# TensorE's instruction stream of a two-layer hybrid decoder: FFN loops written out, and one gate row moved to another PSUM bank

## What is computed

```python
c_act = jax.nn.silu(c)
for l in range(DEPTH):                                   # DEPTH = 2
    mod = (c_act @ ada_w[l] + ada_b[l]).reshape(bsz, 3, 3, D_MODEL)
    h = _modulated_norm(x, norm_g[l, 0], mod[:, 0, 0], mod[:, 0, 1])
    x = x + MACARON_WEIGHT * mod[:, 0, 2][:, None, :] * _swiglu(h, ffn1_w_in[l], ffn1_w_out[l])
    h = _modulated_norm(x, norm_g[l, 1], mod[:, 1, 0], mod[:, 1, 1])
    mix = _token_mixer(h, positions, mix_w_in[l], ...)   # three gated branches
    x = x + mod[:, 1, 2][:, None, :] * mix
    h = _modulated_norm(x, norm_g[l, 2], mod[:, 2, 0], mod[:, 2, 1])
    x = x + MACARON_WEIGHT * mod[:, 2, 2][:, None, :] * _swiglu(h, ffn2_w_in[l], ffn2_w_out[l])
return _rms_norm(x, final_norm_g)
```

## Time and profile before

| | |
|---|---|
| three executions without the profiler | median 1522.95 us (1521.99 to 1523.3) |
| the profiled execution | 1519.81 us, of it span of the instructions 1518.0 us |
| TensorE matmul busy | 1377.5 us (91%), 11953 matmuls |
| VectorE busy | 1014.2 us (67%) |
| ScalarE, GpSimd busy | 650.8 us (43%), 229.5 us (15%) |
| TensorE's share of the chain that ended last | 74% |
| mean granted TensorE clock | 0.975 of full speed |

### The profile page before, as it was taken

One profiled execution on the slowest core, in us unless ns is written; L12 is line 12 of the kernel. 1 busy time (PEld: TensorE's weight loads), 2 busy tenths in 40 slices (PEclk: granted clock), 3 DMA queues, 4 the chain that ended last, 5 costly groups with the idle time before them and its releaser, 6 DMA issues.

```text
span 1518.0 us, 28716 instructions
## 1 busy us (share of the span) xinstructions
PE 1377.5 (91%) x11953; PEld 1272.9 (84%) x11953; DVE 1014.2 (67%) x1327; ACT 650.8 (43%) x943; POOL 229.5 (15%) x256
## 2 busy tenths in 40 slices
PE   1899999978899999999989999897888999999997
PEld 1899978967689988999879998796777898799986
DVE  5777768557555776776677676765656378757756
ACT  2443335465623435443353333536364243643433
POOL 2123200030030001232003230102101100022300
PEclk9999999999999999999999999999899999999999
DMA  8998875824302856997769896792441085599852
GB/s 291 308 291 260 297 259 172 228 56 121 102 4 83 279 167 197 266 267 255 247 205 285 247 299 238 223 243 63 111 112 30 3 241 214 165 273 272 276 208 99
DMA packets 354073, 301.81 MB, mean 199 GB/s; under 512 B 19871, under 2 KB 295344, under 8 KB 353968
## 3 DMA queue, kind: packets, MB, share of 16 engines
q1 hardware_dynamic: 353968, 300.36, 65.7%
HBM read 299.28 MB, written 1.05 MB: 198 GB/s over the span
## 4 chain that ended last, share of the span: by engine, by line
PE 74%; DVE 13%; ACT 6%; DVEq 3%; issue 2%; DMA 1%; ACTq 1%; SPq 0%
PE PS L1520 16%; PE PS L1468 15%; PE PS L1470 14%; PE PS L1469 14%; DVE wl L914 3%; DVE ada_acc L1002 3%; ACT wh L603 3%; PE PS L1891 2%; PE PS L1550 2%; DVE x L961 1%; DMA raw<-in_mix_w_in 1%; DVEq L987 1%; PE PS L1557 1%; PE PS L1510 1%; DVEq L960 1%
## 5 line engine op out<-in xcount | busy, mean ns | idle before, releaser
L603 ACT ACTIVATE wh<-raw 128x1024 fp32r<-128x1024 f32 (+1 forms) x400 | 396.6, 1038 | 604.7 <-PE PS L1470 428.0
L914 DVE TENSOR_TENSOR wl<-raw,wh 128x1024 fp32r<-128x1024 f32 (+1 forms) x400 | 474.2, 1226 | 260.4 <-ACT wh L603 260.4
L1468 PE MATMUL PS<-h_hi,wh 128*128 128x256 f32 x2128 | 608.3, 286 | 26.5 <-DVE h_lo L936 14.1
L1469 PE MATMUL PS<-h_lo,wh 128*128 128x256 f32 x2128 | 600.1, 282 | 0.0
L1470 PE MATMUL PS<-h_hi,wl 128*128 128x256 f32 x2128 | 599.6, 282 | 0.0
L1468 PEld LDWEIGHTS PS<-h_hi,wh 128*128 128x128 f32 x2128 | 409.4, 192 | 31.4 <-issue 24.5
L1469 PEld LDWEIGHTS PS<-h_lo,wh 128*128 128x128 f32 x2128 | 411.3, 193 | 0.6 <-issue 0.5
L1470 PEld LDWEIGHTS PS<-h_hi,wl 128*128 128x128 f32 x2128 | 408.8, 192 | 0.0
L1002 DVE SCALAR_TENSOR_TENSOR ada_acc<-ada_w_ring,cact,ada_acc 128x512 f32<-128x512 f32 x280 | 217.9, 778 | 23.8 <-issue 0.9
L1374 POOL CAST hid_hi<-hf 128x256 fp32r<-128x256 f32 x88 | 64.9, 738 | 432.6 <-DVE hf L973 432.6
L1520 PE MATMUL PS<-wh,hid_hi 128*128 128x512 f32 x320 | 101.8, 399 | 0.0
(11 more groups left out here) (306 smaller groups left out, 1568.3 us busy)
## 6 DMA issues: line engine op xcount, KB each, us to landing
raw<-in_ffn_w_in SPq DMA_DIRECT2D x176, 512.0 KB, 5.4
ada_w_ring<-in_ada_w SPq DMA_DIRECT2D x160, 512.0 KB, 5.2
raw<-in_mix_w_in SPq DMA_DIRECT2D x90, 512.0 KB, 6.4
raw<-in_ffn_w_out SPq DMA_DIRECT2D x44, 1024.0 KB, 5.9
raw<-in_branch_w SPq DMA_DIRECT2D x8, 1024.0 KB, 8.2
raw<-in_mix_w_out SPq DMA_DIRECT2D x8, 1024.0 KB, 4.9
gate_row<-in_ada_b SPq DMA_DIRECT2D x6, 512.0 KB, 6.8
raw<-in_mix_w_in SPq DMA_DIRECT2D x2, 1024.0 KB, 6.2
```

The source lines that it names most:

```text
L603: nc.scalar.activation(wh[:, s % 2, h * n:(h + 1) * n], raw[:, s % 4, h * n:(h + 1) * n], ACT.Copy).then_inc(*one("w_hi"))
L914: V.tensor_tensor(wl[:, s % 2, h * n:(h + 1) * n], raw[:, s % 4, h * n:(h + 1) * n], wh[:, s % 2, h * n:(h + 1) * n].bitcast(F32), ALU.sub ...
L1468: M(out, wh[(slice(None),) + wsl], rhs_h, start=start, stop=False, skip_group_check=True)
L1469: M(out, wh[(slice(None),) + wsl], rhs_l, start=False, stop=False, skip_group_check=True)
```

## The change

TensorE's part of `ffn` is written as a plain `for` over all 22 steps, so `steps`, `still`, the offset `o` and the multiplier `times` are gone everywhere. All waits and addresses on TensorE become constants, and the executed matmuls and their order stay the same. On the other four engines the functions lose an argument that was always zero; their instructions stay as they were, row for row. Beside that, `gate_sum(14)` writes bank 0 in place of bank 4 and loses its wait for `ya_final`.

```diff
-GATE_ROW_BANK = {9: 3, 10: 3, 14: 4, 15: 4, 20: 3, 21: 3}
+GATE_ROW_BANK = {9: 3, 10: 3, 14: 0, 15: 4, 20: 3, 21: 3}
...
-        def steps(eng, first, count, peel=0, tail=0):
...
-            rounds = (count - peel - tail) // 4
-            at0 = first + peel
-            times[0] = rounds
-            with eng.Fori(0, rounds) as i:
-                for u in range(4):
-                    yield at0 + u, lambda n: i * n
-            times[0] = 1
...
-            def split_ready(s, half, o, l):
-                pe.wait_ge(*at("w_split", 2 * s + half + 1 + o(8), l))
+            def split_ready(s, half, l):
+                pe.wait_ge(*at("w_split", 2 * s + half + 1, l))
...
-            def ada_sum(gr, l, o=still, inc=one):
+            def ada_sum(gr, l, inc=one):
 
                 col = ADA_COL.get(gr, 4 * (gr % 16))
-                pe.wait_ge(*at("ada_used", 4 * gr + 4 + o(4), l))
+                pe.wait_ge(*at("ada_used", 4 * gr + 4, l))
                 for i in range(4):
-                    ins = M(PS[:, 7, bass.ds(o(4) + col + i, 1)], acc[:, i * P:(i + 1) * P], onecol,
+                    ins = M(PS[:, 7, col + i:col + i + 1], acc[:, i * P:(i + 1) * P], onecol,
                             start=True, stop=True)
...
-                for s, o in steps(pe, s0, KF, peel=(2, 6)[f]):
-                    j = s - s0
-
-                    pe.wait_ge(*at("hf_ready", f * KF + j - 3 + o(4), l))
+                for j in range(KF):
+                    s = s0 + j
+                    pe.wait_ge(*at("hf_ready", f * KF + j - 3, l))
                     if j == 0:
                         ins = first_slot(s, 0, f * 2 * KD, l)
                     for half in range(2) if j else ():
-                        split_ready(s, half, o, l)
+                        split_ready(s, half, l)
                         ins = in_tile(s, half, j % 4, half * T)
                     ins.then_inc(*one("w_used"))
                     if f == 0 and j % 4 == 0 and j >= 4:
-                        ada_sum(3 + j // 4, l, o)
+                        ada_sum(3 + j // 4, l)
...
                     if j == 9:
-                        pe.wait_ge(*at("ya_final", 1, l))
                         gate_sum(14, l)
```

More of the change, by code:

```diff
@@ L345, in hybrid_trunk @@
         tally.clear()
-        times = [1]
         def sem(name):
@@ L365, in at @@
             return sem(name), l * per_layer.get(name, 0) + v
-        def still(n):
-            return 0
-        def steps(eng, first, count, peel=0, tail=0):
-            if eng is not nc.tensor:
-                for s in range(first, first + count):
-                    yield s, still
-                return
-            for s in range(first, first + peel):
-                yield s, still
-            rounds = (count - peel - tail) // 4
-            at0 = first + peel
-            times[0] = rounds
-            with eng.Fori(0, rounds) as i:
-                for u in range(4):
-                    yield at0 + u, lambda n: i * n
-            times[0] = 1
-            for s in range(at0 + 4 * rounds, first + count):
-                yield s, still
         def ada_place(n, l):
@@ L462, in ffn_loads @@
                         row_loads((l + 1) % DEPTH, j - 4)
-                for s, o in steps(sp, s1, 11, peel=1, tail=2):
-                    j = s - s1
-                    free(s, o, l)
-                    sp.dma_start(rows(s, 2), wout[f][:, bass.ds(l * KF + 2 * j + o(8), 2), :])\
+                for j in range(11):
+                    s = s1 + j
+                    free(s, l)
+                    sp.dma_start(rows(s, 2), wout[f][:, bass.ds(l * KF + 2 * j, 2), :])\
                         .then_inc(sem(f"raw_loaded{s % 4}"), 16)
                     if f == 0 or 1 <= j <= 8:
-                        ada((36, 79)[f] + j, o, l)
+                        ada((36, 79)[f] + j, l)
                     if f == 0 and j == 0:
@@ L534, in _ @@
             for n in range(4):
-                ada(n, still, 0)
+                ada(n, 0)
             sp.dma_start(x[:, :, :], a["x"][0].rearrange("(t p) d -> p t d", p=P)).then_inc(sem("x_loaded"), 16)
@@ L570, in _ @@
                     if s < RW_IN:
-                        ada(47 + s - ATT_IN, still, l)
+                        ada(47 + s - ATT_IN, l)
                 for j in range(12):
                     s = GATE_IN + j
-                    free(s, still, l)
+                    free(s, l)
                     for half in range(2):
@@ L582, in _ @@
                     for n in ADA_LOADS.get(j, ()):
[L583 removed]
+                        ada(n, l)
                 for s in range(BRANCH, FFN2_IN):
[L585 removed]
+                    free(s, l)
                     w, k0, per = (wbr, 2 * (s - BRANCH), 9) if s < MIX_OUT else (wmo, 2 * (s - MIX_OUT), KD)
@@ L676, in _ @@
                     vectors(l)
-                    round_w(0, still, l)
+                    round_w(0, l)
                 norm(l, 0, 1)
@@ L975, in ffn, with ada @@
                     if f == 0 or 4 <= j < 20:
-                        ada((16, 60)[f] + j, o, l)
-                for s, o in steps(dve, s1, 11, peel=1, tail=2):
-                    j = s - s1
+                        ada((16, 60)[f] + j, l)
+                for j in range(11):
+                    s = s1 + j
                     if j < 9:
-                        split(s + 2, o, l)
+                        split(s + 2, l)
                     if 1 <= j <= 8:
-                        ada((37, 79)[f] + j, o, l)
-            def ada(n, o, l, inc=one):
+                        ada((37, 79)[f] + j, l)
+            def ada(n, l, inc=one):
                 q = n % 4
                 dve.drain()
-                dve.wait_ge(sem(f"ada_loaded{q}"), l * (18 * 16) + 16 * (n // 4 + 1) + o(16))
+                dve.wait_ge(sem(f"ada_loaded{q}"), l * (18 * 16) + 16 * (n // 4 + 1))
                 if q == 0 and n:
-                    dve.wait_ge(*at("acc_used", n // 4 + o(1), l))
+                    dve.wait_ge(*at("acc_used", n // 4, l))
                     if n // 4 - 1 in (9, 10, 14, 20):
@@ L1035, in _ @@
             for n in range(16):
-                ada(n, still, 0, inc=once)
+                ada(n, 0, inc=once)
             for l in range(DEPTH):
@@ L1292, in _ @@
                 for j in range(6, 12):
-                    split(GATE_IN + j + 2, still, l)
+                    split(GATE_IN + j + 2, l)
                     for n in ADA_SUMS[j]:
-                        ada(n, still, l)
+                        ada(n, l)
                 dve.wait_ge(*at("gate_ready", 12, l))
@@ L1331, in _ @@
                 merge(2, 0)
-                split(MIX_OUT, still, l)
+                split(MIX_OUT, l)
                 merged_lo(0)
@@ L2002, in _ @@
                     s = BRANCH + kb // 2
-                    split_ready(s, kb % 2 if kb < 8 else 1, still, l)
+                    split_ready(s, kb % 2 if kb < 8 else 1, l)
                     if n == 1 and k == 0:
```

192 lines of the change are left out of this document (95 added, 97 removed).

## The result

The changed kernel is slower. Over 22 executions of each its median is 1527.31 us (1522.17 to 1531.15) against 1521.83 us (1515.44 to 1528.63) for the kernel before; the ratio is 1.0031, 95% interval 1.0019 to 1.0043, that is 4.7 us where a gain of 1.8 was forecast. The profiled execution of the changed kernel took 1527.76 us, its span 1526.0, against 1519.81 and 1518.0. In the new program `mm3` is L1443 to L1445, `ada_sum` L1525, `gate_sum` L1532, `ada` L977, the rounding to `wh` L578, the rest `wl` L889.

What follows compares the result with a forecast made beforehand. TensorE's own stream, its matmuls busy 91% of the span, was taken as the bound; 1.6 us from the `ada_sum` waits plus 0.2 from the gate row made 1.8, median 1522.95 to 1521.2 us, range 1516.0 to 1527.5.

Steps and rivals of the forecast that it cites:

- rival A: Matmuls behind `ada_sum`: more rounds run at the slow pace, 0.63 us net each, median 1529.5 us; chance 0.12 that it shows.
- Branches and register additions: TensorE's feed-forward loops: removing these instructions gains nothing, since matmuls keep their ordinary pace across a branch.
- rival C: TensorE's loops: each of 14 backward branches did cost a 1.0 us fetch, 14 us gained, 1507.1 us; chance 0.04.
- Rival D: DVE's next `ada` is timed by something other than TensorE, so the 0.09 us is given back: 1522.8 us; chance 0.12.
- The wait of `ada_sum`: Inside the loops: with a constant wait each of 18 `ada_sum` starts 0.09 us sooner behind DVE, 1.6 us gained.
- The gate row: `gate_sum(14)`, once per layer: one wait instead of two starts it 0.09 us sooner, 0.2 us gained in all.
- More instruction blocks: nothing: TensorE's instruction queue: 22 more blocks, 94 for 72, cost 0; upper bound 22 us lost, given 0.02.

Runs made afterwards that it cites:

- e1: The kernel before with only the gate row's part of the change (bank 0, no wait for `ya_final`), loops kept; ratio 0.9987 (0.9966 to 1.0009).
- e5: The kernel before, loops kept, with 64 idle semaphore increments at the start of TensorE's program; ratio 1.0028 (1.0012 to 1.0044).
- e10: The kernel before, loops kept, with 192 idle semaphore increments at the start of TensorE's program; ratio 1.0015 (0.9998 to 1.0032).

## Why the prediction was wrong

The measured 1527.31 us lies just inside the range, which had been drawn up to 1527.5 for three quarters of rival A. Something else brought it there, so that is luck, and the forecast of a gain was wrong.

**Branches and register additions: right.** With the long wait a slow round takes 23.81 us in a loop, with branch and register instructions, and 23.79 written out: at most 0.02 us a round. **The rule of the Trainium skill behind rival C** did not come about, as the unbroken pace had said; it speaks of targets outside the instruction window, and nothing was loaded for the first loop. **Rival D** is level by number, but not for its reason: the gain was not given back by DVE, as each round keeps its 0.08 us.

**The wait of `ada_sum`: right in its size.** 0.05 us behind DVE in place of 0.15, idle 0.17 in place of 0.27. Over a round it is 0.08 us, 18 of them 1.4 us in place of 1.6. It was real, and was outweighed.

**The gate row: right.** Its matmul starts 0.06 us behind DVE in e1, 0.15 before, and alone it changed nothing in the time that could be measured.

**"More instruction blocks: nothing": this step failed.** 94 blocks was right and the 1.0 us each too, but the step asked only how many more there are and whether a feed-forward takes them at full pace. It looked at a stretch in which no load is waited for. The blocks also share the DMA engines with the one weight load on which the end of the gate slots hangs, and they must arrive in time where matmuls are short. Both depend on the place of each block, and writing out four loops moved every block behind them. The rows stood there: the wait of 1.34 us ahead of `gate_sum(14)` should have been followed up to ACT's 4.7 us wait for a load, and the next question should have been what else is in flight. Instead the upper bound, 22 more blocks at 1.0 us, got a chance of 0.02 as if all or none would count. What the runs showed in its place is e5: 64 idle instructions, no block more, and 4.3 us.

The size: in the changed kernel the two late gate rows show 1.1 + 0.9 = 2.1 us; the measured loss is 4.7. Over all kernels with up to 224 increments, what idles before `gate_sum(14)` plus the stalls goes along with the measured difference (correlation 0.78, 16 kernels), but the difference grows 1.6 times as fast. A third to a half of the loss by place is therefore not located. The attention part between 305 and 430 us differs most between profiles, 125.0 us before and up to 132.6, but the longest there (131.0 and more) are those with the most time at a low granted clock, so that stretch shows nothing of the place.

**The pace, rival A: half right.** I put 0.12 on more slow rounds showing. Over one profile each, seven looped executions had 4, 8, 5, 7, 6, 4 and 4 of 14 rounds slow, mean 5.4; twelve written-out ones 6 to 11, mean 8.6 (standard deviations 1.6 and 2.0). That is 3.2 rounds more, at 0.62 us each (the prediction had 0.63) 2.0 us: it outweighs the gain of 1.6 (1.4 and the gate row's 0.2), and would explain why the changed kernel at a good place is level (1.0001, 1.0000, 0.9995) and not 0.1% faster. A change of 0.1% is too small to be told from none by these intervals, so that account is argued. The prediction named exactly this balance (three more slow rounds), but took the shifted restart for the cause. Three profiles with the long wait, written out, speak against that: 6, 9 and 10 slow, the same. Which property of written-out code does it stays open.

## What to carry to other kernels

An edit that adds or removes instructions ahead of a sensitive stretch moves the boundaries of the instruction blocks in it, and in this kernel that alone was worth 0.3%, more than the edit's own terms. So before believing in a gain or loss of this size, run both versions with 64, 128 and 192 idle instructions at a place where the engine waits, and compare the means. When a forecast says that a transfer is hidden, look for it beside the loads that are waited for, not where none is.

## What the runs showed of the hardware

One instruction block in mid-flight (2.7 to 5.2 us behind the issue) lengthens a half-load of a gate slot to 7.4 to 7.8 us, where it takes 6.2 to 7.0 without, but for 7.2 and 7.3 us in two of 31 cases; one that comes 5.3 us into it or later does not. The block itself, 16 KB, takes about 1.0 us.

A block boundary in the chain of 64x64 matmuls can cost 0.3 to 0.9 us where it is reached 2.3 to 2.9 us behind the last block's load (14 cases in seven kernels; e10 has one reached so and free), and nothing that shows where that load is 3 us or more back.

A semaphore increment on TensorE takes 0.12 us (64 in 7.93). An `ada_sum` with one constant wait starts 0.05 us behind its releaser, with two waits 0.145 us, even where the second was satisfied long ago.

Executions of one kernel scatter by some 12 us, and that goes with the mean granted clock: the kernel before took 1515.38 us at 0.976 and 1528.07 at 0.967, over all runs about 0.9 us for each 0.001, without one execution of it at 0.925 that took 1537.81. The clock was no different between the two kernels, so it explains the scatter and not the result.

The two paces, 0.113 and 0.118 us for each matmul, appeared in every kernel, looped or not: slow rounds of four steps take 0.62 us more than fast ones.
